# Convolution taps gathered by VectorE in SBUF, and the query rows ahead of the keys, in a hybrid decoder kernel

## The reference

```python
def conv_module(h, ctx, w_pw1, b_pw1, w_dw, b_dw, ln_g, ln_b, w_pw2, b_pw2):
    a = h @ w_pw1 + b_pw1
    a = a[..., :D_MODEL] * jax.nn.sigmoid(a[..., D_MODEL:])
    full = jnp.concatenate([ctx, a], 1)
    y = depthwise_conv(full, w_dw) + b_dw          # 31 taps per channel
    y = jax.nn.silu(layer_norm(y, ln_g, ln_b))
    return y @ w_pw2 + b_pw2, full[:, -30:]

def mla_project(h, pos, w_down, g_q, g_kv, w_uq, w_uk):
    d = h @ w_down
    q_lat = rms_norm(d[..., :384], g_q)
    ckv = rms_norm(d[..., 384:640], g_kv)
    kr = rope(d[..., 640:], pos)
    q = q_lat @ w_uq                                # 8 heads of 128 + 64
    q_abs = einsum('bthn,chn->bthc', q[..., :128], w_uk)
    return q_abs, rope(q[..., 128:], pos), ckv, kr
```

## Time and profile before

| what | us |
|---|---|
| median of 3 runs | 3004.7 (3002.46 to 3007.76) |
| the profiled execution | 3006.55 |
| its span | 3004.8 |
| TensorE busy | 2908.9 |
| VectorE busy | 1643.8 |
| GpSimd busy | 1699.8 |
| convolution loop, first taps to first sums of the norm | 864.3 to 988.4 |
| latent attention, query transposes to first query row | 1540.0 to 1553.8 |

### The profile page before, as it was taken

The page is one execution under the profiler, slowest core; times in us unless marked ns, Lnnn a source line. Parts: engine busy times, 40 slices in busy tenths (PEclk is TensorE's granted clock), DMA queues, the critical chain, the costliest instruction groups (busy, mean ns, idle before and its releaser), DMA issues.

```text
span 3004.8 us, 53453 instructions
## 1 busy us (share of the span) xinstructions
PE 2908.9 (97%) x21220; PEld 2681.8 (89%) x21220; DVE 1643.8 (55%) x3121; ACT 926.0 (31%) x1813; POOL 1699.8 (57%) x1177
## 2 busy tenths in 40 slices
PE   5999999999999999999989999999999999999997
PEld 4789999999976799999976689999997999999997
DVE  3153684636563784636565548463663536856363
ACT  2220142414230352414233315241423301425141
POOL 2546546868655445857620044685764465468685
PEclk8999999999999999999999999999999999999999
DMA  6643434333344434444321334444422333222332
GB/s 229 249 112 92 124 116 162 99 113 112 100 121 134 170 116 160 151 136 148 97 64 44 95 124 136 148 146 141 140 79 85 96 91 103 67 82 85 88 96 74
DMA packets 450485, 354.84 MB, mean 118 GB/s; under 512 B 26120, under 2 KB 424832, under 8 KB 437933
## 3 DMA queue, kind: packets, MB, share of 16 engines
q1 hardware_dynamic: 435744, 324.79, 35.1%
q10 hardware_dynamic: 14493, 26.63, 3.0%
HBM read 337.86 MB, written 5.25 MB: 114 GB/s over the span
## 4 chain that ended last, share of the span: by engine, by line
PE 81%; DVE 7%; issue 3%; ACT 3%; POOL 2%; DVEq 1%; DMA 1%; POOLq 1%; ACTq 1%; SPq 1%
PE pb L1153 79%; POOL w_lo L1004 1%; DMA ada_first<-in_ada_w 1%; DVE part L2778 1%; ACT h_hi L2145 1%; POOLq L1003 1%; ACT hf L2145 1%; DVE pb L2797 1%; PE pb L1989 1%; DVE xa L2804 0%; DVE h_lo L2828 0%; DVE pr L3107 0%; PE pb L1266 0%; DVE part L2773 0%; ACTq L2442 0%
## 5 line engine op out<-in xcount | busy, mean ns | idle before, releaser
L1001 POOL TENSOR_SCALAR w_hi<-w_raw 128x1024 fp32r<-128x1024 f32 (+2 forms) x272 | 295.9, 1088 | 751.0 <-DMA w_raw<-in_gmlp_w_in 275.7
L1004 POOL TENSOR_TENSOR w_lo<-w_raw,w_hi 128x1024 fp32r<-128x1024 f32 (+2 forms) x272 | 653.1, 2401 | 45.0 <-issue 45.0
L1153 PE MATMUL pb<-a_hi,w_hi 128*128 128x288 f32 x2176 | 593.8, 297 | 2.1 <-DVEq L3392 1.9
L1153 PE MATMUL pb<-a_lo,w_hi 128*128 128x288 f32 x2176 | 588.4, 294 | 0.0
L1153 PE MATMUL pb<-h_hi,w_hi 128*128 128x288 f32 x2144 | 563.9, 299 | 18.0 <-DVE pr L3084 7.9
L1153 PE MATMUL pb<-h_lo,w_hi 128*128 128x288 f32 x2144 | 545.6, 296 | 0.0
L1046 POOL TENSOR_TENSOR w_lo<-w_raw,w_hi 128x512 fp32r<-128x512 f32 x288 | 382.3, 1349 | 180.0 <-DVE s_raw L3049 83.2
L1153 PEld LDWEIGHTS pb<-h_hi,w_hi 128*128 128x128 f32 x2144 | 392.8, 188 | 33.4 <-DVE pr L3084 10.9
L1153 PEld LDWEIGHTS pb<-a_hi,w_hi 128*128 128x128 f32 x2176 | 408.3, 188 | 8.8 <-POOL a_lo L1071 4.2
L1153 PEld LDWEIGHTS pb<-a_lo,w_hi 128*128 128x128 f32 x2176 | 408.6, 188 | 0.8
L1153 PEld LDWEIGHTS pb<-h_lo,w_hi 128*128 128x128 f32 x2144 | 389.5, 189 | 0.0
(11 more groups left out here) (379 smaller groups left out, 4875.9 us busy)
## 6 DMA issues: line engine op xcount, KB each, us to landing
ada_w<-in_ada_w SPq DMA_DIRECT2D x80, 1024.0 KB, 7.7
w_raw<-in_ffn_w_gate SPq DMA_DIRECT2D x88, 512.0 KB, 3.8
w_raw<-in_ffn_w_up SPq DMA_DIRECT2D x88, 512.0 KB, 3.8
w_raw<-in_gmlp_w_in SPq DMA_DIRECT2D x64, 512.0 KB, 4.2
w_raw<-in_ffn_w_down SPq DMA_DIRECT2D x64, 512.0 KB, 4.3
w_raw<-in_gmlp_w_out SPq DMA_DIRECT2D x32, 512.0 KB, 4.7
...
```

The costliest lines, as they stand in the source:

```text
L1001: nc.gpsimd.tensor_scalar(w_hi[:, s, 0:w], w_raw[:, s, 0:w], 1.0, 1.0, ALU.mult, ALU.mult).then_inc(split_hi, 1)
L1004: nc.gpsimd.tensor_tensor(w_lo[:, s, 0:w], w_raw[:, s, 0:w], w_hi[:, s, 0:w].bitcast(F32), ALU.subtract).then_inc(split_lo, 1)
L1153: return nc.tensor.matmul(out, lhsT, rhs, start=start, stop=stop)
```

## The change

In the convolution, a table `PE_TAPS` says how many of the eight groups TensorE keeps: 6, 5, 5, 5, 5, 6, 8, 8. GpSimd makes only these diagonals. VectorE does the other taps (7, 11, 11, 11, 11, 7 of them) on 512 prompt rows in the output buffer `yc` in SBUF, before it waits for TensorE's sums, and adds these with the bias at the end. The running sums of the previous tile move between the two halves of `gated_in`.

In the latent attention, the query rows come ahead of the keys. ScalarE writes the upper part of the query blocks (`query_upper`), VectorE the lower (`query_lower`), `latents` falls into `scale_keys` and `turn_keys` with the copies of the query rows between, and the keys' transposes go to the aux banks behind the ten query-row products. ScalarE copies them after it has issued the four output DMAs of the keys.

```diff
@@ -117,6 +117,7 @@
 XW = SEQ + QT * (TG - 1)
+PE_TAPS = (6, 5, 5, 5, 5, 6, TG, TG)
@@ -445,7 +446,8 @@
         kt_ready = sem("kt_ready")
-        kt_copied = sem("kt_copied")
+        ql_turned = sem("ql_turned")
+        ql_upper = sem("ql_upper")
         ql_scaled = sem("ql_scaled")
@@ -755,6 +757,7 @@
         turn_at = []
+        ql_at, keys_at = [], []
@@ -1011,8 +1014,8 @@
                     last = nc.gpsimd.tensor_tensor(
-                        diag[:, m % 2, q], mask4[:].unsqueeze(1).to_broadcast([P, TG, QC]),
-                        w4[:, q, m, :].unsqueeze(2).to_broadcast([P, TG, QC]), ALU.mult)
+                        diag[:, m % 2, q, 0:PE_TAPS[m]], mask4[:].unsqueeze(1).to_broadcast([P, PE_TAPS[m], QC]),
+                        w4[:, q, m, 0:PE_TAPS[m]].unsqueeze(2).to_broadcast([P, PE_TAPS[m], QC]), ALU.mult)
                 last.then_inc(diag_ready, 1)
@@ -1764,10 +1767,10 @@
-                    for g in range(TG):
+                    for g in range(PE_TAPS[m]):
                         for q in range(QT):
                             last = mm(out[QC * q:QC * (q + 1), 0:c1 - c0], diag[:, m % 2, q, g, :],
-                                      x4[:, m % 2, q, QT * g + c0:QT * g + c1], g == 0, g == TG - 1)
+                                      x4[:, m % 2, q, QT * g + c0:QT * g + c1], g == 0, g == PE_TAPS[m] - 1)
                     return last
@@ -1855,25 +1858,33 @@
                 pe.wait_ge(ql_scaled, 1)
+                ql_at.append(X.n)
                 for k in range(3):
-                    transposes([(tt * P, dtok[:, tt, k * P:(k + 1) * P]) for tt in range(4)])
-                    transposes([(0, dtok[:, 4, k * P:(k + 1) * P])])
-                pe.wait_ge(kv_ready, 1)
-                pe.wait_ge(acc_free, G.n + BANKS)
-                for k in range(3):
-                    for tt in range(TT):
-                        rows = (ckv[:, tt, k * P:(k + 1) * P] if k < 2
-                                else kr2[:, tt, :, :].rearrange("p a n -> p (a n)"))
-                        out = pb[:, k, tt * P:(tt + 1) * P] if tt < 4 else pb[:, 3, k * P:(k + 1) * P]
-                        last = nc.tensor.transpose(out, rows, ident[:])
-                    last.then_inc(kt_ready, 1)
-                pe.wait_ge(kt_copied, 5)
+                    for tts in (range(4), (4,)):
+                        b = aux_bank()
+                        for tt in tts:
+                            last = nc.tensor.transpose(pb[:, b, tt % 4 * P:(tt % 4 + 1) * P],
+                                                       dtok[:, tt, k * P:(k + 1) * P], ident[:])
+                        last.then_inc(ql_turned, 1)
+                        X.up()
                 pe.wait_ge(lat_ready, 1)
...
                                   (lambda k: ql_hi[:, k, token_tile(tt)], lambda k: ql_lo[:, k, token_tile(tt)]))
+                pe.wait_ge(kv_ready, 1)
+                pe.wait_ge(aux_free, X.n + BANKS)
+                keys_at.append(X.n)
+                banks = [BANKS + (X.n + i) % BANKS for i in range(BANKS)]
+                for k in range(3):
+                    for tt in range(TT):
+                        rows = (ckv[:, tt, k * P:(k + 1) * P] if k < 2
+                                else kr2[:, tt, :, :].rearrange("p a n -> p (a n)"))
+                        out = pb[:, banks[k], tt * P:(tt + 1) * P] if tt < 4 else pb[:, banks[3], k * P:(k + 1) * P]
+                        last = nc.tensor.transpose(out, rows, ident[:])
+                    last.then_inc(kt_ready, 1)
+                X.up(BANKS)
@@ -1903,6 +1914,8 @@
                         absorb(h - 1)
+                    else:
+                        pe.wait_ge(aux_free, X.n + BANKS)
                     expand(aux_bank(), lambda c: ukr[:, c, h * P:(h + 1) * P], lambda c: ckvT[:, c, 0:SEQ])
@@ -2515,13 +2528,18 @@
+                def query_upper(k):
+                    b_p, b_s = [BANKS + (ql_at[0] + 2 * k + i) % BANKS for i in range(2)]
+                    act.wait_ge(ql_turned, 2 * k + 2)
+                    fn(ql_hi[:, k, 0:SEQ], pb[:, b_p, :], ACT.Copy)
+                    fn(ql_hi[:, k, SEQ:], pb[:, b_s, NS:P], ACT.Copy).then_inc(ql_upper, 1)
+                for k in range(2):
+                    query_upper(k)
                 square_sums(1, KVR, QR, range(4, TT))
-                for k in range(3):
-                    act.wait_ge(kt_ready, k + 1)
-                    fn(ckvT[:, k, 0:SEQ] if k < 2 else krT[:, 0:SEQ], pb[:, k, :], ACT.Copy).then_inc(kt_copied, 1)
-                fn(ckvT[:, :, SEQ:], pb[:, 3, 0:2 * P].rearrange("p (k t) -> p k t", k=2)[:, :, NS:], ACT.Copy
-                   ).then_inc(kt_copied, 1)
-                fn(krT[:, SEQ:], pb[:, 3, 2 * P + NS:3 * P], ACT.Copy).then_inc(kt_copied, 1)
+                query_upper(2)
                 act.wait_ge(kv_ready, 1)
@@ -2530,6 +2548,15 @@
                               ).then_inc(kv_out, 16)
+                key_banks = [BANKS + (keys_at[0] + i) % BANKS for i in range(BANKS)]
+                for k in range(3):
+                    act.wait_ge(kt_ready, k + 1)
+                    fn(ckvT[:, k, 0:SEQ] if k < 2 else krT[:, 0:SEQ], pb[:, key_banks[k], :], ACT.Copy
+                       ).then_inc(aux_free, 1)
+                ps = pb[:, key_banks[3], :]
+                fn(ckvT[:, :, SEQ:], ps[:, 0:2 * P].rearrange("p (k t) -> p k t", k=2)[:, :, NS:], ACT.Copy)
+                fn(krT[:, SEQ:], ps[:, 2 * P + NS:3 * P], ACT.Copy)
+                act.drain().then_inc(aux_free, 1)
                 G.up(10 + 3 * HEADS)
@@ -3354,18 +3381,31 @@
                     if m < KT - 2:
-                        for h in range(2):
-                            gated_in(m + 2, h, h)
-                        dve.drain().then_inc(rows_ready, 1)
-                        complete(m + 2)
+                        gated_in(m + 2, 0, 0)
                     if m:
...
                         last_.then_inc(q_done, 1)
+                    if m < KT - 2:
+                        gated_in(m + 2, 1, 1)
+                        dve.drain().then_inc(rows_ready, 1)
+                        complete(m + 2)
                     sample_taps(m)
-                    v.tensor_scalar(one(yc, m, slice(0, SEQ)), pb[:, aux(), :], one1(par, m, C_DW), None, ALU.add
-                                    ).then_inc(aux_free, 1)
+                    y = one(yc, m, slice(0, SEQ))
+                    for w in range(QT * PE_TAPS[m], CW):
+                        if w == QT * PE_TAPS[m]:
+                            v.tensor_scalar(y, full[:, m % 3, w:w + SEQ], wdT[:, m, w:w + 1], None, ALU.mult)
+                        else:
+                            v.scalar_tensor_tensor(out=y, in0=full[:, m % 3, w:w + SEQ], scalar=wdT[:, m, w:w + 1],
+                                                   in1=y, op0=ALU.mult, op1=ALU.add)
+                        dve.drain()
+                    sums_ = pb[:, aux(), :]
+                    if PE_TAPS[m] < TG:
+                        v.scalar_tensor_tensor(out=y, in0=sums_, scalar=one1(par, m, C_DW), in1=y,
+                                               op0=ALU.add, op1=ALU.add).then_inc(aux_free, 1)
+                    else:
+                        v.tensor_scalar(y, sums_, one1(par, m, C_DW), None, ALU.add).then_inc(aux_free, 1)
                     dve.drain().then_inc(yc_ready, 1)
@@ -3455,8 +3495,7 @@
-                def latents(n, t0, t1):
+                def scale_keys(n, t0, t1):
@@ -3464,6 +3503,9 @@
+                def turn_keys(t0, t1):
@@ -3481,10 +3523,20 @@
-                def evac_latents(ks):
-                    for k in ks:
-                        for cols, src in ((slice(0, SEQ), slice(0, SEQ)), (slice(SEQ, TOK), slice(NS, P))):
-                            split(ql_hi[:, k, cols], ql_lo[:, k, cols], pb[:, aux(), src]).then_inc(aux_free, 1)
+                def query_lower(k):
+                    dve.wait_ge(ql_upper, k + 1)
+                    for cols, src in ((slice(0, SEQ), slice(0, SEQ)), (slice(SEQ, TOK), slice(NS, P))):
+                        v.tensor_tensor(ql_lo[:, k, cols], pb[:, aux_of(X.n), src], ql_hi[:, k, cols].bitcast(F32),
+                                        ALU.subtract).then_inc(aux_free, 1)
+                        X.up()
+                def query_rows(n):
+                    c, tt = divmod(n, TT)
+                    dve.wait_ge(acc_ready, G.n + 1)
+                    v.tensor_copy(qrt[:, tt, c * 256:(c + 1) * 256], pb[:, G.n % BANKS, 0:256]).then_inc(acc_free, 1)
+                    G.up()
@@ -3499,19 +3551,21 @@
                             scale_queries()
-                        if tt == TT - 2:
-                            latents(2, 0, 4)
-                evac_latents((0,))
-                latents(3, 4, TT)
+                for k in range(3):
+                    query_lower(k)
+                dve.drain().then_inc(lat_ready, 1)
+                scale_keys(2, 0, 4)
+                for n in range(2):
```

(17 more changed lines are left out.)

## The result

The changed kernel takes 3032.2 us (median of 4 runs, 3028.5 to 3041.6) against 3003.6 for the kernel before, run beside it: a ratio of 1.0098, 95% interval 1.0081 to 1.0116, so it is 28.6 us slower.

The account below looks back on a forecast made before the run. TensorE, busy 97% of the span, was taken to bound the kernel. Profiled execution 3006.55, +45 for the convolution, +2 for the low clock, -7 for the latent part, made 3046.6, so a median of 3045 us; range 3018 to 3056.

Parts of the forecast that it names:

- Own chains: Convolution loop: VectorE's own work per tile, without waits for GpSimd, put at 16 us, some 17 with ScalarE handshakes.
- The walk, +45: Convolution: engines' lists walked in program order, VectorE and GpSimd taking turns; stage ends 45 us later, TensorE's 11.4 included.
- splits lengthened by 0.7: Convolution, profile after: GpSimd's weight splits were expected to last 0.7 us longer.
- TensorE's 11.4 us: Convolution: TensorE's gain from dropped tap groups, 12 groups and half of tile 5's two, 11.4 us.
- Low clock, +2: End of the convolution: last taps and sums start at the 1.2 GHz level after TensorE's gaps, adding 2 us.
- Latent part, -7: Latent attention: query rows start 8.8 us earlier, key transposes behind them cost 1.9, gain 7 us (3.5 at half clock).
- TensorE's ten rows end at 1555.8: Latent attention: VectorE's key work ends near 1554, before TensorE's ten query rows end at 1555.8, covering the wait.
- (a): Rival, convolution: VectorE keeps the ports through a whole chain of taps; +25 -7, so 3023 to 3025; chance 0.16.
- (b): Rival, convolution: taps do not exclude GpSimd's operations, TensorE keeps its 11.4 and gains 7; 2987 us; chance 0.08.
- (c): Rival, whole kernel: it cancels, with waits of some 30 us; no difference beyond 0.2%; chance 0.03.
- (d): Rival, convolution: taps longer than 0.75 us and low clock in TensorE's work; over 3056 us; chance 0.07.
- (e): Rival, latent attention: the new order does nothing, the wait only moves to the keys; 3052; inside the forecast's 0.66.

## Why the prediction was right, and where its sizes were off

The sign and the mechanism hold: slower, because VectorE's taps and GpSimd's operations exclude each other, and the tiles then wait for VectorE's gating. The time came out 13 us under the forecast of 3045, inside the range. By the spans, 40.0 us were forecast and 24.2 measured: the convolution took 13.6 less than 45 + 2, 5.7 came from places not forecast, and the latent part gave 3.5 less than 7. That last shortfall hides a part of the first error, which is luck and not a merit of the sum.

**Own chains.** Estimated 16 to 17 us a tile for VectorE, measured 16.6 in the changed kernel and 16.9 with the taps in PSUM. A tap is 0.75 us instead of 0.70 and 0.82 instead of 0.78 with its drain; the first 0.48 instead of 0.40. The forecast had priced 0.75 at 2 us more, so this error is small and has the other sign.

**The walk, +45.** Measured +33.4, with the low clock in it; this is the term that was mis-sized. The walk had tile 5 done at 1024.9 (929.9 + 20 + 27 + 20 + 28), and it was done at 1015.0, 9.9 earlier. VectorE's waits for GpSimd in each tile, by the walk and by the trace (what each operation takes over its length alone):

| tile | 0 | 1 | 2 | 3 | 4 | 5 |
|---|---|---|---|---|---|---|
| walk | 5.6 | 21 | 4 | 11 | 4 | 15 |
| trace | 7.9 | 15.5 | 4.0 | 8.1 | 4.0 | 12.9 |

So the waits in tiles 2 and 4 were right, and the excess lies in tile 1 first, then in tiles 3 and 5, where GpSimd has most to do. I had let each turn cost both sides the other's whole length, and forecast splits lengthened by 0.7. In the trace the ends of two turns lie over each other: a `w_hi` beside taps lasts 1.48 instead of 1.05, a `w_lo` 2.57 instead of 2.40, and in tile 1 a diagonal (0.43 alone) and a tap (0.75 alone) follow each other every 0.86 us:

```profile
911.41 0.79 DVE L3400 SCALAR_TENSOR_TENSOR yc<-full,wdT,yc 128x512 f32<-128x512 f32 x1
912.27 0.79 DVE L3400 SCALAR_TENSOR_TENSOR yc<-full,wdT,yc 128x512 f32<-128x512 f32 x1
```

```profile
910.75 0.90 POOL L1016 TENSOR_TENSOR diag<-mask,w 128x160 f32<-128x160 f32 x1
```

Beside tile 1's taps eight GpSimd operations (the product, four diagonals, `w_hi`, `w_lo`, `w_hi`) are 3.2 us longer together, where 0.7 each makes 5.6. That explains 2.4 of the 5.5 us there; the rest, and how tiles 3 and 5 divide, stays open.

Two sums of the walk were off by themselves. GpSimd's work a tile with the 0.16 between the splits is 13.1 us, not 12.8, and the waits named tile by tile add up to 60.6 us, not 67.

**Where the waiting lies.** I had put the waits at 67 us and the taps' mean at about 1.7 us. The taps' mean is 1.16, and all waits come to some 54 us: in the stretch from 860 to 1025 the taps wait 21 us, the bias 18 (20.2 for seven of them, 0.26 each alone), the running sums and ring copies some 13, and the first taps 1. The prediction names the bias only as a part of VectorE's own work, not as something that is held, and an edit of a few lines moves it out of the way.

**TensorE's 11.4 us.** Not seen in the changed kernel, but real: three taps a tile gain 4.4 of 4.4, and seven in PSUM 6.0 to 8.0 of 8.8, by the two traces (first sums at 982.9 and 980.9 against 989.0).

**Low clock, +2.** Right in size for the last taps, inside the 33.4: they take 6.57 us instead of 4.09, at a granted clock of 0.50 over 1015 to 1019. The sums behind them are at full clock again (0.72 us, before 0.75).

**Latent part, -7.** The start of the rows was right within 0.3 us (1545.0 forecast, 1544.72 measured on the scale of before). The step that failed is "TensorE's ten rows end at 1555.8", with nothing in their way: the tenth block waits 2.24 for VectorE, which turns the last keys first and is held 2.2 us by GpSimd's splits there. The prediction had applied the turns to the convolution alone. Together with half clock in the key transposes that leaves 3.5 in this execution, the lower end that I gave; where the clock holds it is 5.5 in the trace and 6.5 in the medians.

**The rest.** A gain of 5.7 us elsewhere was not forecast; 2.62 of it are a wait of before that TensorE no longer meets.

**Rivals.** (a), keeping the ports through a chain, gives a time near the measured one for a wrong reason: its 3023 to 3025 against 3032.2, but at 904 to 922 GpSimd gets its turn between taps all along, with `prod` starting at 906.23 in the middle of the chain. (b) falls by the taps themselves. (c) and (d) fall by the time, 1.0098 and 3032.2. (e) falls by the latent part alone, 0.9978 (0.9968 to 0.9988).
